# Two RWKV blocks that share tokens, the norm's factor behind the gate products, and the memory's stage beside the gates

## The reference, cut to what matters

```
n = rmsnorm(x, attn_norm)
u_gdn, u_mlstm, u_rglru, u_rwkv = split(n @ w_in)
mix = concat([gated_deltanet(u_gdn), mlstm(u_mlstm), rglru_block(u_rglru), rwkv7_time_mix(u_rwkv)])
x = x + mix @ w_out
x = x + (silu(n2 @ w_gate) * (n2 @ w_up)) @ w_down ;  x = rmsnorm(x, final_norm)
```

## Time and profile before

| | |
|---|---|
| median of 3 runs | 2434.52 us (2432.32 to 2436.34) |
| profiled execution, own time | 2434.96 us |
| its span, first to last instruction | 2433.2 us |
| PE busy | 2395.0 us, 98% of the span |
| DVE busy | 1433.0 us, 59% |
| ACT busy | 1129.4 us, 46% |
| HBM traffic | 433 MB read, 182 GB/s over the span |
| chain that ended last | PE 90%, DVE 6%, ACT 2% |

### The profile page before, as it was taken

How to read it: one execution, slowest core, us unless ns; L and a number is a source line. 1 busy time by engine, 2 the same in 40 slices (tenths; PEclk the granted TensorE clock), 3 DMA queues, 4 the chain that set the end, 5 groups by cost and what they waited for, 6 DMA issues and landing times.

```text
span 2433.2 us, 32292 instructions
## 1 busy us (share of the span) xinstructions
PE 2395.0 (98%) x13430; PEld 1991.1 (82%) x13430; DVE 1433.0 (59%) x1855; ACT 1129.4 (46%) x1424; POOL 117.5 (5%) x83
## 2 busy tenths in 40 slices
PE   8899999999999999999999999999999999999998
PEld 7687888878888888888888888888888888888887
DVE  4866658577755555555555575555446655555555
ACT  6645435554554444444434464445444455344444
POOL 0110111220000000000000040000000000000000
PEclk9999999999999999999999999999999999999999
DMA  9543344645555555555555566555545545555564
GB/s 327 192 140 122 122 140 162 215 160 182 198 188 178 189 190 190 190 190 190 182 191 185 186 204 231 188 173 174 173 156 189 169 144 171 193 190 184 194 242 141
DMA packets 245618, 445.65 MB, mean 183 GB/s; under 512 B 7393, under 2 KB 72545, under 8 KB 242657
## 3 DMA queue, kind: packets, MB, share of 16 engines
q1 hardware_dynamic: 241984, 423.65, 52.9%
q0 software_dynamic: 2912, 19.40, 2.1%
q10 hardware_dynamic: 576, 0.53, 0.1%
HBM read 433.07 MB, written 10.49 MB: 182 GB/s over the span
## 4 chain that ended last, share of the span: by engine, by line
PE 90%; DVE 6%; ACT 2%; issue 1%; DMA 1%; SPq 0%; ACTq 0%; DVEq 0%
PE pp L644 24%; PE pp L646 24%; PE pp L645 24%; PE pp L673 7%; PE pp L674 3%; DVE ringL L1956 2%; PE ps L603 2%; DVE AR L2461 1%; DMA raw<-in_w_in 1%; PE ps L1250 1%; PE ps L1264 1%; PE ps L777 1%; ACT ringH L1338 1%; PE ps L830 0%; DVE AR L1964 0%
## 5 line engine op out<-in xcount | busy, mean ns | idle before, releaser
L1338 ACT CAST ringH<-raw 128x1024 fp32r<-128x1024 f32 x779 | 814.8, 1050 | 1002.2 <-PE pp L646 870.4
L1956 DVE TENSOR_TENSOR ringL<-raw,ringH 128x1024 fp32r<-128x1024 f32 x779 | 952.3, 1242 | 462.3 <-ACT ringH L1338 461.4
L644 PE MATMUL pp<-ringH,nS 128*128 128x512 f32 x1376 | 545.1, 396 | 3.9 <-DVE ringL L1956 2.8
L646 PE MATMUL pp<-ringH,nS 128*128 128x512 f32 x1376 | 536.5, 390 | 0.0
L645 PE MATMUL pp<-ringL,nS 128*128 128x512 f32 x1376 | 536.0, 390 | 0.0
L673 PE MATMUL pp<-nS,ringH 128*128 128x512 f32 x992 | 367.4, 411 | 10.4 <-DVE ringL L1956 5.4
L644 PEld LDWEIGHTS pp<-ringH,nS 128*128 128x128 f32 x1376 | 258.4, 188 | 59.7 <-DVE ringL L1956 6.1
L646 PEld LDWEIGHTS pp<-ringH,nS 128*128 128x128 f32 x1376 | 258.2, 188 | 54.6
L645 PEld LDWEIGHTS pp<-ringL,nS 128*128 128x128 f32 x1376 | 258.6, 188 | 51.1 <-issue 0.2
L674 PE MATMUL pp<-nS,ringL 128*128 128x256 f32 x992 | 280.5, 283 | 0.0
L644 PE MATMUL pp<-ringH,xS 128*128 128x512 f32 x704 | 277.2, 394 | 0.0
(11 more groups left out here) (392 smaller groups left out, 1957.7 us busy)
## 6 DMA issues: line engine op xcount, KB each, us to landing
raw<-in_w_in SPq DMA_DIRECT2D x189, 1024.0 KB, 5.1
raw<-in_ffn_w_gate SPq DMA_DIRECT2D x44, 1024.0 KB, 5.2
raw<-in_ffn_w_up SPq DMA_DIRECT2D x44, 1024.0 KB, 5.2
raw<-in_ffn_w_down SPq DMA_DIRECT2D x44, 1024.0 KB, 5.1
raw<-in_w_out SPq DMA_DIRECT2D x32, 1024.0 KB, 5.2
raw<-in_w_mem_kv SPq DMA_DIRECT2D x16, 1024.0 KB, 5.3
raw<-in_w_proj_a SPq DMA_DIRECT2D x8, 1024.0 KB, 5.1
raw<-in_w_proj_m SPq DMA_DIRECT2D x8, 1024.0 KB, 5.2
```

Source lines behind the costliest of these rows:

```text
L644: mm(o, XH[:, ts(j)], WH, first, False)
L646: t_of[0] = mm(o, XL[:, ts(j)], WH, False, last)
L1338: e.copy(ringH[:, h % NSPL, 0:nh * cols], raw[:, u % NRAW, h0 * cols:(h0 + nh) * cols]).then_inc(*hi.tick(h))
L1956: tt2(ringL[:, h % NSPL, o], raw[:, u % NRAW, h0 * cols:(h0 + nh) * cols], ringH[:, h % NSPL, o].bitcast(F32), SUB).then_inc(*lo.tick(h))
```

## The change

RWKV's weight columns come as an input of their own, `w_rwkv`, in the order in which they are used, 8 KB in a row for each partition and unit. w0 and w1 are worked on in turns over the same slices of tokens: w0 rows 0 to 3, w1 rows 0 to 3, w0 4 to 7, w1 4 to 7, and then w0's and w1's upper halves. The lead of the ring is two halves until the sixth half instead of the third. "norm" has only eight halts (24 steps of 256 instead of 40); the squares, the root and `factor` move into "gates", behind the gate products. `gateS` moves onto x_dim's place, so that its filling waits for the last slice of x. "gates" has eight halts with paces 4, 3, 3, 3, 3, 3, 3, 1, and `both` joins it with `beside_rwkv` as soon as w0 is done. "mem" has three empty halts first and then four groups of four slices instead of eight of two. On SP's queue `mem_dim` goes ahead of the masks.

```diff
@@ course
     L.run("turn")
-    L.weave(L.stage("gates"), 2)
     side = beside_rwkv(L)
+    L.weave(L.both(L.stage("gates"), side, "w0"), 2)
     while not L.done("w3"):
         next(side)
         L.step(4)
     L.weave(L.both(L.stage("rwkv"), side, "w3"), 1.5)
@@ layouts
+    units = [[(q, k) for q in range(2) for k in range(4 * h, 4 * h + 4)] for h in range(2)] + [
+        [(q, k) for k in range(8, 16)] for q in range(2)] + [
+        [(q, k) for k in range(8 * h, 8 * h + 8)] for q in range(2, 7) for h in range(2)]
+    wr = np.stack([np.concatenate([first[q, k] for q, k in u], 1) for u in units])
@@ program
-        gateS = alias("gateS", 0, [128, 4096])
+        gateS = alias("gateS", SC, [128, 4096])
+        for q, k in [(0, 0), (1, 0), (0, 4), (1, 4), (0, 8), (0, 12), (1, 8), (1, 12)] + [
+                (q, k) for q in range(2, 7) for k in range(0, 16, 4)]:
+            rwkv_half(blocks[q], range(k, k + 4))
@@ tensor, norm
-                yield 0
-                for _ in range(7):
-                    yield 1
-                yield 3
-                yield 4
-                yield 5
-                e.wait_ge(s_i, 16)
-                factor("nx", nx_p, nx_v, rx)
-                yield 1
+                for pace in (0, 3, 1, 3, 2, 1, 1, 1):
+                    yield pace
@@ tensor, gates
-                yield
+                yield 4
                 e.wait_ge(*nx_v.at("lo", 15))
                 e.wait_ge(*gt_v.at("gl"))
...
                 yield 3
                 yield 3
+                e.wait_ge(s_i, 16)
+                factor("nx", nx_p, nx_v, rx)
+                yield 3
+                yield 3
+                yield 3
...
-                yield 2
+                yield 3
...
-                yield
+                yield 1
@@ tensor, mem
-                for _ in range(8):
+                for _ in range(3 + 4):
                     yield 3
@@ scalar and vector, unit
-                    while sent[0] < min(s.half + (NSPL if s.half > 2 else 2), len(halves)):
+                    while sent[0] < min(s.half + (NSPL if s.half > 5 else 2), len(halves)):
@@ sync, params
                 e.dma_start(prm[:, 16:], I["params"][:, 16:]).then_inc(s_p, 16)
+                e.dma_start(mem_dim, I["mem_dim"]).then_inc(s_mt, 16)
+                e.dma_start(csg[:, :], I["csg"]).then_inc(s_c, 16)
                 e.dma_start(cm[:, 128:], I["cmask"][:, 128:]).then_inc(s_c, 16)
                 e.dma_start(crst[:, :], I["crst"]).then_inc(s_c, 16)
-                e.dma_start(csg[:, :], I["csg"]).then_inc(s_c, 16)
                 for tt in range(2):
                     e.dma_start(memk[:, tt, :], I["mem_2"][0, ts(tt), :]).then_inc(s_m[tt], 16)
-                e.dma_start(mem_dim, I["mem_dim"]).then_inc(s_mt, 16)
```

More of the change, by code:

```diff
@@ L1486, in norm, with gates @@
                 e.wait_ge(s_an, 16)
-                square = squared(nx_a, xtok, small[:, 112:114], s_xt, v2(MU + 988, 2048))
-                yield from to_hi("nx", x_dim, {c.start: s for c, s in zip(x_parts, s_x)}, nx_a, lambda k: pc("attn_norm", k), lambda k: nS[:, k, 0, :], lambda n: None, square, ())
+                landed = {c.start: s for c, s in zip(x_parts, s_x)}
+                for k in range(16):
+                    if k in landed:
+                        e.wait_ge(landed[k], 16)
+                    act(nS[:, k, 0, :], x_dim[:, k, :], ACT.Copy, scale=pc("attn_norm", k)).then_inc(*nx_a.tick("hi", k))
+                    if k in (0, 1, 3):
+                        high_first(min(k, 2))
+                        sent[0] = 1
+                    if k % 2:
+                        yield
+            def gates(L):
+                square = squared(nx_a, xtok, small[:, 112:114], s_xt, v2(MU + 988, 2048))
+                gH = gateS[:, 0:2048].rearrange("p (k g c) -> p k g c", k=16, g=4)[:, :, :, 0:4]
+                e.wait_ge(*nx_v.at("lo", 15))
+                e.copy(gateS[:, 0:2048], small[:, 127:128].broadcast_to([128, 2048])).then_inc(*gt_a.tick("z"))
+                e.wait_ge(s_w, 16)
+                e.wait_ge(*gt_a.now())
+                e.copy(gH, wsm.rearrange("p k (g h) -> p k g h", g=4)).then_inc(*gt_a.tick("gh"))
                 yield
@@ L1523, in mem @@
             def mem(L):
+                for _ in range(3):
+                    yield
                 Eq, lam = small[:, 44:48], prm[:, pcol["rglru_lambda"]:pcol["rglru_lambda"] + 4]
+                square = squared(me_a, memk, small[:, 116:118], s_m, v2(SC + 2048, 2048))
                 e.wait_ge(s_p, 16)
@@ L1528, in mem @@
                 act(Eq, Eq, ACT.Exp, scale=-1.0).then_inc(*rg_a.tick("E"))
[L1530 to L1537, removed]
+                e.wait_ge(*gt_p.at("g"))
+                e.wait_ge(s_mt, 16)
+                for g in range(4):
+                    if g >= 2:
+                        e.wait_ge(s_mh[g - 2], 16)
+                    for k in range(4 * g, 4 * g + 4):
+                        act(mSt[g % 2][:, k % 4, 0, :], mem_dim[:, k, :], ACT.Copy, scale=pc("norm_mem_g_2", k)).then_inc(
+                            *me_a.tick("hi", k))
+                    if g in (1, 2):
+                        square(g - 1)
+                    yield
                 yield
@@ L2061, in unit, with mean_square @@
                         ring.free(drain_v.now(), "h", g, b)
[L2064 to L2072, removed]
-                            low_first(min(k, 2))
-                            cut[0] = 1
-                    yield
-            def factor(key, mp, ma, mv, c0, rows):
+            def mean_square(ma, mv, c0):
                 ss, r = small[:, c0:c0 + 2], small[:, c0 + 2:c0 + 4]
@@ L2081, in factor, with one_over @@
                 tsc(r, ss, 1.0 / D, 1e-6, MUL, ADD).then_inc(*mv.tick("ms"))
-                yield
+            def one_over(ma, mv, c0):
+                r = small[:, c0 + 2:c0 + 4]
                 e.wait_ge(*ma.at("rt"))
                 e.reciprocal(r, r).then_inc(*mv.tick("r"))
-                if key == "me":
-                    yield
+            def factor(key, mp, mv, rows):
                 e.wait_ge(*mp.at("r"))
@@ L2105, in gates @@
                 yield
+                yield
+                mean_square(nx_a, nx_v, 112)
+                one_over(nx_a, nx_v, 112)
+                yield
+                factor("nx", nx_p, nx_v, rxb)
+                own(nx_v)
                 zr, bs, gc, e_, m_ = grows
-                e.wait_ge(s_h, 16)
-                e.wait_ge(s_c, 48)
                 e.wait_ge(*gt_p.at("g"))
@@ L2185, in mem @@
                 yield
-                yield from factor("me", me_p, me_a, me_v, 116, rmb)
+                mean_square(me_a, me_v, 116)
+                yield
+                one_over(me_a, me_v, 116)
+                yield
+                factor("me", me_p, me_v, rmb)
                 yield
```

82 lines of the change are left out of this document (42 added, 40 removed).

## The result

The changed kernel takes 2493.97 us (median of 4 runs, 2492.42 to 2498.82) against 2435.01 for the kernel before. The ratio is 1.0249, with a 95% interval of 1.0236 to 1.0262: 59 us slower, where 50 were forecast. Lines of kernel.py moved: L673 and L674 are now L689 and L690, L679 is L695, L1065 is L1079, and L817, L825 and L830 are L831, L839 and L844. VectorE's lines moved by up to 25.

What follows compares the result with a forecast made beforehand. The prediction took PE as the bound, busy for 2395.0 of 2433.2 us. Bare chain 50 + deltanet 8 - head 8 = +50 us on 2434.96 gave 2485, with a range of 2455 to 2515.

Steps and rivals of the forecast that it cites:

- The count of portions: Filler in RWKV's halts: RWKV starts with 58 portions, asks for 146.8, and nothing fills it from the 33rd of 71 halts.
- The bare chain: RWKV without filler, from the first half-head's output part through the second half-head: 73.7 us at full clock, +50 taken.
- The choice of the middle: Bare chain's term: 50 us taken between full and half clock, since no row shows the clock in an inversion without filler.
- the ends: Bare chain's term: 36 us idle added if the clock stays full, 65 us at half clock.
- The upper end: Bare chain at half clock: PE's products on it take twice as long, about 103 us instead of 73.7, so 65 added.
- The rule of the Trainium skill: Bare chain's clock: work shorter than its waits falls back to half rate; 65 instead of 50, total 15 us longer.
- The deltanet's stage: Behind RWKV: o's first gate opens about three halts late and the last three halts are bare; 8 us lost, 5 to 12.
- The head: First 120 us: at most 23 us to win; 8 us gained taken, bounds 5 lost and 17 gained.
- The range: Whole kernel: 2455 to 2515 us, leaving out 2 in 10.
- The wait of the scan: Scan of the gates in the head, 3.1 us of PE's wait before; expected gone in the profile after.
- what was named against the head: Head: same work and transfers come earlier, 341 GB/s beside 362 with a full queue; ACT and the gates' chain can wait.
- The price of nothing for the 8 KB rows: Loads of `w_rwkv`: 8 KB rows in place of 1 KB rows priced at nothing.

Runs made afterwards that it cites:

- e1_mem_only: The changed kernel with only the memory's stage joined to the gates and mLSTM released where it was before; 2441.67 us, ratio 1.0036 to the kernel before.
- e2_mlstm_first: The kernel before with only the new order of mLSTM, run to its end before RWKV's first halt; 2483.58 us, ratio 1.0206 to the kernel before.
- e9_mem_lag: e5_lead4 with VectorE's slices of the memory and GpSimd's transfers of them one halt later; 2440.55 us, ratio 1.0034 to the kernel before.
- e5_lead4: e1_mem_only with the ring of weight halves four ahead from the third half, not the sixth; 2437.98 us, ratio 1.0017 to the kernel before.
- e8_loads_early: e1_mem_only with the loads of parameters, masks and memory issued ahead of the wait for the third unit's slot; 2441.95 us, ratio 1.0044 to the kernel before.
- e6_1kb_rows: e1_mem_only with RWKV's weights laid out in rows of 1 KB, not 8 KB; 2443.16 us, ratio 1.0041 to the kernel before.
- e11_gdn_pace: e5_lead4 with the deltanet's stage taking 3.2 portions a halt, not 3.5; 2440.06 us, ratio 1.0023 to the kernel before.
- e10_lag_early: e9_mem_lag with the seven loads of parameters, masks and memory issued ahead of the third unit's wait; 2447.28 us, ratio 1.0054 to the kernel before.
- e12_both_holes: e9_mem_lag with mean square and reciprocal ahead of the lambda terms and 3, 3, 3 portions before the memory's factor; 2430.95 us, ratio 0.9989 to the kernel before.

## Why the prediction was right, and what it got wrong

**The count of portions** was right, and it decided the sign. mLSTM's heads end near 240 us, not 220, but before the first inversion; dense steps stop inside RWKV, and r0 comes behind it. e1_mem_only and e2_mlstm_first show the cause by undoing it and by doing it alone.

**The bare chain** was put at 73.7 us at full clock and about 103 at half. It is 93.7 us long, at half clock for most of it (a mean of 0.58). PE's own products were estimated at 38 us at full clock; the run with dummy products gives 37.1. The choice of the middle was too low for the stretch itself: 50 taken, 56 lost, with the ends at 36 and 65. The upper end was too high, because it let each of PE's products on the chain take twice as long. Between 430 and 432 us, at a clock of 0.50, a batch of 32 products of L844 takes 1.92 us; at full clock it took 1.10 (L830 in the earlier trace rows), and PE's busy time in the stretch rose from 37.1 to 62.1. Both rise by about 1.7 times, not 2. With 1.7 in place of 2 the prediction's own sum gives 73.7 + 0.7 x 29.3, about 94 us, instead of 103 (an estimate; the 73.7 was never measured).

The stretch is not the whole price. Ahead of it PE idles for only 1.4 us from 120 us on, where the kernel before idled for 5.6 from 120 us to r0. The prediction didn't count such a gain. Up to r0's start the order costs 36 us alone (e2_mlstm_first) and 46 inside the change (48.6 - 3.0). So the 50 lies between a stretch that lost more and a net price that is smaller; that it is so near is partly luck.

The rule of the Trainium skill that the prediction named ("TensorE: Matmul & The Clock Gate", section on HAM oscillation) says that work shorter than its waits keeps the array falling back to half rate. The clock was indeed low (0.58 from 369 to 462 us), but the rule's condition is not met here: PE worked for 62.1 us and waited for 31, and in a level of the inversion it works for about 3.7 us between waits of 0.95. By that rule the term was 65; the 56 measured lies between it and the 50 taken.

**The deltanet's stage** was put at +8, with 5 to 12. From r0's start to the end the order costs 13.7 us alone and 11.5 inside the change (15.2 - 3.7), so this term was too small and its upper bound at best just held. The mechanism was there: o's first gate opens late. RG-LRU, whose output opens it, has its scan only at 610.2 us and writes its output from 620.5 on; from 604.6 to 621.3 there is no dense step, and 6.5 us are idle in three waits, at a clock of 0.83 from 600 to 640. Bare chain and deltanet together were 58 in the sum and are 52 by e1_mem_only and 50 by e2_mlstm_first.

**The head** is the step that failed: "I take 8 us gained, with bounds of 5 lost and 17 gained". The part of the change without the new order costs 8 (5.6 to 11.9 by its interval), so this term is 16 us off in the sum and beyond its own bound. About 3 of the 8 are lost up to r0's start and about 4 behind it, in the deltanet's stage, where the prediction put nothing for this part. The range held all the same, because the overestimate of the other terms (58 for 50 to 52) went the other way and the range was wide.

Three things were wrong in the term. The wait of the scan was taken as covered by more portions, where the scan itself came later: it was queued behind the memory's slices on VectorE (e9_mem_lag brings the wait from 6.5 to 3.0 us). The short lead of the ring to the sixth half was not priced at all; e5_lead4 gives about 4 us for it. And VectorE was expected near full from 30 to 70 us, while it is busy for 18.55 of these 40: it waits in order, it has no lack of time. One thing was right in it: the norm's factor waits no more. But the memory's factor got a wait of its own, 1.9 us here and 7.2 in e9_mem_lag. Of what was named against the head, earlier loads (e8_loads_early) change nothing. The price of nothing for the 8 KB rows holds within what the runs can tell (e6_1kb_rows).

**What stays open.** Why e1_mem_only, with mLSTM in its old place, loses 3.7 us from r0's start on. Dense steps wait there for VectorE's cuts, but the sparser pace of e11_gdn_pace gives nothing back. The phase of the steps against the halts is argued, not shown. Why e10_lag_early is 6.7 us slower than e9_mem_lag is not shown either. How the 56 us of the stretch would fall with a full clock and nothing added was not measured either.

## What to carry to other kernels

Where a serial stage is hidden by independent work that is dealt out in portions, the portions are the resource: count them from the gate backwards before moving anything, and follow every generator to its end (here a `yield from` ran a whole stage early). Thinner portions can't replace missing ones. A wait that goes at one place in an engine's in-order queue can come back one link later: e9_mem_lag took 3.5 us from one wait and got 7.2 at the next, and only e12_both_holes, which dealt with that place too and put more portions there, came out just ahead of the kernel before. And compare runs at one point of the work (here r0's start), not only in fixed windows.

## What the runs showed of the hardware

At half clock the small products didn't take twice as long. One product of 64x64 by 32 columns took 291 ns from its start to its end, against 219 at full clock, and 64x64 by 64 columns 317 (from 424 to 440 us, at a clock of 0.50) against 224: a third to two fifths more. But they overlap, and what counts for a chain is the batch: 32 of the first kind took 1.10 us at full clock and 1.92 at half, 1.7 times.

```profile
430.14 1.92 PE L844 MATMUL ps<-AR 64*64 64x32 f32 x32 [0.95 <-DVE AR L2269]
```

PE's busy time over the whole stretch rose by nearly the same factor, from 37.1 to 62.1 us. In the stretch the clock stayed low even where PE was busy for most of a window, as here in the changed kernel:

```profile
408.00:440.00 32.00, 23.68 (x532) 21.84 (x524) 11.99 (x33) 2.47 (x6) 0.00 (x0) 0.55 0.01 3
```

With the dummy products between them the same small products ran at a clock of 1.00:

```profile
408.00:440.00 32.00, 31.65 (x596) 22.94 (x594) 13.06 (x37) 1.75 (x5) 0.00 (x0) 1.00 0.01 3
```
